# Attention of a decoder trunk: half of the last down group carried into the first attention steps, the first projection of a group issued after the last scores, and the end reordered

## The chip, the cores and the metric

The kernel runs on one core of a Trainium2 chip. The time is the device time of one execution in microseconds (us). Before the change the median of 3 runs is 2696.46 us (2696.24 to 2699.46). TensorE (PE) multiplies, VectorE (DVE) and ScalarE (ACT) do element work, GpSimd (POOL) helps them, and SyncE (SP) issues most transfers.

## The reference, cut to what matters

Two decoder layers over 1024 tokens of width 1024. The first mixes tokens by retention, the second by sliding-window attention; each is followed by a squared-ReLU MLP with 4096 hidden columns. The change lies in the seam between the MLP of layer 0 and the attention of layer 1, in the attention, and in the seam from it to the MLP of layer 1.

```
h = rmsnorm(x, norm_mix[1])
q, k, v = split(h @ w_in)                # 16 query heads in 4 groups, one key/value head per group, 64 wide
q = rope(rmsnorm(q, q_gain)); k = rope(rmsnorm(k, k_gain))
scores = q k^T * 64**-0.5, masked to the current and the previous block of 128 keys
probs = softmax([scores, sink])[..., :-1]
x = x + (probs @ v) @ w_out
h = rmsnorm(x, norm_mlp[1])
x = x + square(relu(h @ w_up)) @ w_down
```

## The kernel before, in words

Everything is float32. A product of two matrices is three matmuls (`product`, L475 to L483): each operand is split into a rounded part (hi, written by ACT) and a remainder (lo, written by DVE), and hi*hi, lo*hi and hi*lo are summed in PSUM. The residual stream xT lies transposed in SBUF: 8 pieces of 128 features by 1024 tokens, handled as 16 tiles of 128x512; tiles 0 to 7 are the first half of the tokens, tiles 8 to 15 the second.

The engines run their own instruction lists in the order written in the code, and wait for each other by counting semaphores. So the order of the work is written out by hand, and an instruction that waits holds up all behind it on its engine.

**Down groups.** An MLP's second matrix is applied in 16 groups of 256 hidden columns. A group is 16 tiles: `down` (L638) makes 6 matmuls of 512 columns on PE, `add` (L648) adds the result to xT on DVE. In the last group of layer 0 (`finish_dve`, L654) the next RMSNorm starts too: for each tile ACT writes hT_hi (L521) and a square (L516), DVE hT_lo (`norm_low`, L527), and POOL sums the squares (`norm_pool`, L535), 7 adds for each half. A few tiny matmuls sum over the partitions (`norm_stat_pe`, L544), and `norm_rstd` on DVE makes the reciprocal root in 10 small steps, each of which waits for the one before; other work is put between them.

**Attention.** `sw_steps` runs 4 groups of 8 blocks (128 queries each). The work on a block is cut into stages, and step s of a group runs the stages of several blocks:

- a (block s): 24 matmuls of 384 columns, the projection of q, k and v. ACT then squares and copies it (L1850, L1857, L1860), DVE takes the variance of each head and its root (L1964 to L1973, L463 to L473) and scales it (L1981, L1987), POOL rotates it (L2007 to L2017).
- b (block s-1): 4 transposes, after the rotation. ACT and DVE split the result (L1875, L1876, L1908, L1909).
- c (block s-1): 6 matmuls of 512 columns, the scores. DVE masks them and takes the row maximum (L1929, L1938, L1945 to L1949), ACT the exponentials (L1891, L1893), DVE the sum and a scaling (L1955, L1957, L2023), ACT the other half of the scaling (L1867).
- d, e (block s-2): 8 transposes and 12 matmuls of 256 columns, the weighted values (L1883, L1915, L1901, L2029).
- f (from s = 6 on, 2 tiles per step, also in the next group's first six steps): a down group with the output matrix, each tile followed by an `add`.

At a group's step 0, stages b to f still work for the blocks 6 and 7 of the group before; that is called a turn here. There are three. Projection weights of the next group are split at step 7 (L1758, L1763), the output matrix at steps 4 and 6, on DVE before the adds and before the end of the softmax.

**The end.** In the last group f makes 4 tiles per step from step 6 on. Its tiles 0 to 7 are finished by step 7; the last two steps (TT and TT+1, `drain_pe`, `drain_act`, `drain_dve`, `between_*`) finish the softmax of the last blocks, start the MLP of layer 1 (`p_pe`, `edge_act`, `edge_low`) and do tiles 8 to 15. Then `plain_act`, `plain_dve` and `up_pe` do the first eight results of the up product in the order `P_ORDER`; the norm's factor goes to memory and is read back broadcast (`rb_sp`), and the first ReLUs (`p_relu_dve`, L849) wait for it. The up product goes on (`u_pe`) once four ReLUs have freed a bank.

Of the kernel before, what the change touches and what calls it, by code (L numbers as in the profile page):

```python
# [85 lines left out]
P_ORDER = ((11, 0), (21, 0), (11, 1), (12, 0), (22, 0), (21, 1), (12, 1), (22, 1))  # L86
# [41 lines left out]
def trunk(nc, x_in, positions, norm_mix, norm_mlp, w_up, w_down, ret_in, ret_out, sw_in, q_gain,  # L128
          k_gain, sinks, sw_out, c_ident, c_causal, c_mask, c_head, c_freq, c_freq_row, out, y_dram, x_dram, a_dram, r_dram):
    ctx = ExitStack()  # L130
    with ctx:
# [365 lines left out]
        def sq_slot(n, i):  # L497
            return squares[:, i % 2, :] if n == 3 else xn[:, 0, (i % 2) * HALF:(i % 2 + 1) * HALF]
# [31 lines left out]
        def norm_pool(pool, n, half):  # L530
            for k in range(1, KT):
# [3 lines left out]
                pool.tensor_tensor(ss_of(half), ss_of(half), sq_slot(n, i), ALU.add).then_inc(n_ss, 1)  # L535

        def norm_stat_pe(pe, n, half):
# [3 lines left out]
            for part in ((0, 1) if n % 2 else (half,)):  # L541
                for j in range(4):
                    c = 4 * part + j
                    last = pe.matmul(ps[:, BSTAT, c:c + 1], ss_of(part)[:, j * P:(j + 1) * P], causal[:, P - 1:P],  # L544
                                     start=True, stop=True)
            last.then_inc(n_st, 1)

        def norm_rstd(dve, n, half, meanwhile=()):
# [5 lines left out]
            else:  # L554
                dve.wait_ge(n_st, RS_AT[n] - 2 + half + 1)
                total = ps[:, BSTAT, cols]
# [96 lines left out]

        def finish_dve(dve, g, between):  # L654
# [324 lines left out]
        def plain_dve(dve, layer, begin):  # L979
# [7 lines left out]
            for kk in range(4):  # L987
                t_dve(dve, layer, 6, kk)
            norm_rstd(dve, 2 * layer + 1, 0, [lambda kk=kk: b_lo_dve(dve, layer, 6, kk) for kk in range(4)] +
# [5 lines left out]
            p_lo_dve(dve, layer, 7)  # L995
# [17 lines left out]
        def plain_act(act, layer, begin, final):  # L1013
# [5 lines left out]
            for i in (5, 6):  # L1019
                for kk in range(4):  # L1020
                    b_hi_act(act, layer, i, kk, final)
            p_hi_act(act, layer, 7)
# [140 lines left out]
        def dn_pe(pe, layer, g, b, tile_done=None):  # L1163
            pe.wait_ge(w_lo, wc(PC_D[layer]) + 4 * g + 4)
            for m in range(TILES):
# [6 lines left out]
        def down_pe(pe, layer, tile_done):  # L1172
# [4 lines left out]
            dn_pe(pe, layer, D_LAST, 1, tile_done)  # L1177
# [590 lines left out]
        def a_pe(pe, g, t):  # L1768
            i = TT * g + t
            if t == 0:  # L1770
                pe.wait_ge(w_lo, WC_SW + SW_PIECES * g + 4)
                if isinstance(g, int) and g == 0:
                    pe.wait_ge(x_add, TILES * DG_SW - 3)
# [7 lines left out]
        def b_pe(pe, g, t):  # L1781
# [3 lines left out]
            if isinstance(g, int) and g == SW_KV - 1 and t >= TT - 2:  # L1785
                pe.wait_ge(x_add, TILES * (DG_SW + g) + 4 * (t - TT + 3))
            else:
                wait(pe, x_add, TILES * DG_SW + 2 * max(i - 5, 0) if isinstance(i, int) else TILES * DG_SW + 2 * (i - 5))
# [15 lines left out]
        def d_pe(pe, g, t):  # L1804
            i = TT * g + t
            pe.wait_ge(sw_prob, 2 * (i + 1))
            for s in range(2):
                wait(pe, sw_plo, 2 * (i - 1) + s + 1)
                for hh in range(4):
# [3 lines left out]
        def e_pe(pe, g, t):  # L1813
# [3 lines left out]
            if isinstance(g, int) and i == 0:  # L1817
                pe.wait_ge(n_var, 5)
# [9 lines left out]
        def f_pe(pe, g, q, c):  # L1828
            if c == 0:
                pe.wait_ge(sw_olo, TT * g + 4 * (q // 4) + 4)  # L1830
# [87 lines left out]
        def mask_half(dve, g, t, j):  # L1918
# [4 lines left out]
            if isinstance(g, int) and i == 0 and j == 0:  # L1923
                dve.wait_ge(sw_mask, 16)
                dve.wait_ge(n_ss, sums(2, 1, KT - 1))
# [108 lines left out]

        def drain_pe(pe, s):
# [12 lines left out]

        def drain_act(act, s):
            if s == TT - 1:  # L2050
                act.wait_ge(a_mm, TT * SW_KV)
                for m in range(4):
# [491 lines left out]
```

## Time and profile before

| | |
|---|---|
| median of 3 runs | 2696.46 us |
| the profiled execution's own time | 2694.79 us |
| its span, first to last instruction | 2693.1 us |
| mean granted TensorE clock | 0.982 of 2.4 GHz |
| PE busy | 2581.0 us (96%) |
| DVE busy | 1794.4 us (67%) |
| ACT busy | 931.8 us (35%) |
| POOL busy | 289.0 us (11%) |

The attention takes about 430 us of the span, from 1566 to 2008 us. The page is an average over stages with different limits; the change touches only the stretch from 1544 to 2062 us, so the stretches and single instructions there are what is to be read. Matmul rows overlap: a row's duration is longer than the distance to the next (0.39 against 0.227 us for 512 columns), so the starts are to be used.

### The profile page before, as it was taken

To read this page: it belongs to the slowest core of one execution; us is meant where nothing else is said; L and a number is where in the kernel's file an instruction comes from. 1 tells how busy PE (TensorE), PEld (TensorE's weight loads), DVE (VectorE), ACT (ScalarE), POOL (GpSimd) and SP (SyncE) were. 2 spreads that over 40 slices of the span, in tenths; PEclk is the share of its full clock that TensorE was granted. 3 is DMA by queue.
4 is the path that set the end of the run, shared out by engine and by line. 5 is a ranking of instruction groups with operands and counts; after the bars stand their busy time and mean duration, and the time that the engine had idled before them with its cause. 6 is when DMAs were issued, how large, how long until landed. Compare 5 with 4: busy or idle time off the path is not lost.

```text
span 2693.1 us, 36897 instructions
## 1 busy us (share of the span) xinstructions
PE 2581.0 (96%) x11929; PEld 2153.9 (80%) x11929; DVE 1794.4 (67%) x3397; ACT 931.8 (35%) x1732; POOL 289.0 (11%) x344
## 2 busy tenths in 40 slices
PE   8999999999999999999999988999888999999999
PEld 6878878878788888877888877888767888788887
DVE  7555454454667876666667788888867666576675
ACT  6232332322312544431112255555554444321111
POOL 2102011020000300000000043322320000000000
PEclk8999999999999999999999999999989999999999
DMA  6012120121333333343222201001113323522222
GB/s 206 28 48 67 52 68 16 48 71 47 134 101 97 116 123 117 119 150 121 95 100 93 87 21 40 17 24 40 35 52 118 125 90 112 195 94 99 96 93 86
DMA packets 161735, 231.77 MB, mean 86 GB/s; under 512 B 21681, under 2 KB 103889, under 8 KB 161618
## 3 DMA queue, kind: packets, MB, share of 16 engines
q1 hardware_dynamic: 159314, 226.10, 25.5%
q10 hardware_dynamic: 2304, 4.20, 0.4%
q8 instruction: 63, 1.03, 0.2%
q14 instruction: 54, 0.44, 0.0%
HBM read 171.53 MB, written 58.73 MB: 85 GB/s over the span
## 4 chain that ended last, share of the span: by engine, by line
PE 79%; DVE 11%; issue 5%; ACT 3%; DMA 1%; POOL 0%; DVEq 0%; ACTq 0%; SPq 0%
PE ps L480 25%; PE ps L482 25%; PE ps L481 25%; ACT xn L1891 1%; DVE xT L652 1%; DVE wqg_lo L449 1%; PE ps L1286 1%; PE ps L1287 1%; PE ps L1288 1%; DVE hT_lo L527 1%; DVE smax L1938 1%; DVE pT_lo L1915 1%; DVE hss L1971 1%; PE ps L1334 0%; DVE ws_lo L1763 0%
## 5 line engine op out<-in xcount | busy, mean ns | idle before, releaser
L652 DVE TENSOR_TENSOR xT<-ps,xT 128x512 f32<-128x512 f32 x704 | 482.1, 689 | 269.5 <-PE ps L482 269.2
L480 PE MATMUL ps<-aT_hi,wd_hi 128*128 128x512 f32 x1408 | 557.1, 396 | 21.9 <-DVE xT L652 19.3
L481 PE MATMUL ps<-aT_lo,wd_hi 128*128 128x512 f32 x1408 | 552.5, 392 | 0.0
L482 PE MATMUL ps<-aT_hi,wd_lo 128*128 128x512 f32 x1408 | 552.3, 392 | 0.0
L480 PE MATMUL ps<-bh,uw_hi 128*128 128x512 f32 x880 | 344.1, 391 | 10.3 <-DVE uw_lo L740 8.6
L482 PE MATMUL ps<-bh,uw_lo 128*128 128x512 f32 x880 | 343.4, 390 | 0.0
L481 PE MATMUL ps<-bl,uw_hi 128*128 128x512 f32 x880 | 343.3, 390 | 0.0
L480 PEld LDWEIGHTS ps<-aT_hi,wd_hi 128*128 128x128 f32 x1408 | 266.7, 189 | 79.9 <-issue 12.8
L482 PEld LDWEIGHTS ps<-aT_hi,wd_lo 128*128 128x128 f32 x1408 | 266.6, 189 | 56.1
L481 PEld LDWEIGHTS ps<-aT_lo,wd_hi 128*128 128x128 f32 x1408 | 266.8, 190 | 53.8
L442 ACT ACTIVATE aT_hi<-raw 128x1024 fp32r<-128x1024 f32 x80 | 80.8, 1052 | 604.8 <-PE ps L482 591.4
L480 PEld LDWEIGHTS ps<-bh,uw_hi 128*128 128x128 f32 x880 | 165.8, 188 | 45.9 <-DVE uw_lo L740 9.2
L481 PEld LDWEIGHTS ps<-bl,uw_hi 128*128 128x128 f32 x880 | 165.8, 188 | 34.1
L482 PEld LDWEIGHTS ps<-bh,uw_lo 128*128 128x128 f32 x880 | 165.6, 188 | 34.2
L1551 DVE BATCH_NORM_STATS2 bn<-ps 128x6 f32<-128x512 f32 x32 | 22.4, 699 | 157.0 <-PE ps L482 157.0
L1891 ACT ACTIVATE xn<-xn,nmax 128x256 f32<-128x256 f32 x128 | 63.6, 499 | 143.3 <-DVE sdif L1949 143.3
L758 DVE TENSOR_TENSOR uw_lo<-raw,uw_hi 128x512 fp32r<-128x512 f32 x112 | 77.0, 690 | 52.3 <-ACT uw_hi L753 51.5
L449 DVE TENSOR_TENSOR aT_lo<-raw,aT_hi 128x1024 fp32r<-128x1024 f32 x80 | 97.3, 1218 | 15.1 <-ACT aT_hi L442 15.1
L758 DVE TENSOR_TENSOR uw_lo<-us,uw_hi 128x512 fp32r<-128x512 f32 x84 | 58.0, 692 | 73.7 <-ACT uw_hi L753 73.7
L480 PE MATMUL ps<-wqg_hi,hT_hi 128*128 128x512 f32 x256 | 100.2, 391 | 4.9 <-DVE wqg_lo L449 4.9
L480 PE MATMUL ps<-wv_hi,hT_hi 128*128 128x512 f32 x256 | 102.2, 399 | 0.0
L480 PE MATMUL ps<-ws_hi,hT_hi 128*128 128x384 f32 x256 | 88.7, 347 | 11.7 <-DVE ws_lo L1763 6.7
(285 smaller groups left out, 4709.5 us busy)
## 6 DMA issues: line engine op xcount, KB each, us to landing
raw<-in_w_up SPq DMA_DIRECT2D x64, 512.0 KB, 6.0
raw<-in_w_down SPq DMA_DIRECT2D x64, 512.0 KB, 3.5
raw<-a_dram SPq DMA_DIRECT2D x64, 512.0 KB, 3.2
raw<-in_ret_w_in SPq DMA_DIRECT2D x48, 512.0 KB, 5.3
a_dram<-upost SPq DMA_DIRECT2D x64, 256.0 KB, 2.1
a_dram<-xn SPq DMA_DIRECT2D x64, 256.0 KB, 2.0
xT<-x_dram SPq DMA_DIRECT2D x24, 512.0 KB, 5.9
y_dram<-xn SPq DMA_DIRECT2D x32, 256.0 KB, 2.3
```

Source lines behind the costliest of these rows:

```text
L442: act.activation(dst, src, ACT.Copy).then_inc(w_hi, 1)
L449: dve.tensor_tensor(dst, src, hi.bitcast(F32), ALU.subtract).then_inc(w_lo, 1)
L480: pe.matmul(bank, ah, bh, start=(begin and i == 0), stop=False, skip_group_check=not begin)
L481: pe.matmul(bank, ah, bl, start=False, stop=False, skip_group_check=not begin)
L482: last = pe.matmul(bank, al, bh, start=False, stop=(i == len(pairs) - 1), skip_group_check=not begin)
L527: dve.scalar_tensor_tensor(hT_lo[:, k, cols], xT[:, k, cols], gain(2, k), hT_hi[:, k, cols].bitcast(F32), ALU.mult, ALU.subtract).then_inc ...
L652: dve.tensor_tensor(xT[:, k, cols], ps[:, banks[m % len(banks)], :], xT[:, k, cols], ALU.add).then_inc(x_add, 1)
L758: dve.tensor_tensor(uw(uw_lo, s % URING), weight(i, q), uw(uw_hi, s % URING).bitcast(F32), ALU.subtract).then_inc(u_lo, 1)
L1286: pe.matmul(bank, wh, hT_hi[:, k, cols], start=(k == 0), stop=False)
L1287: pe.matmul(bank, wh, hT_lo[:, k, cols], start=False, stop=False)
L1288: last = pe.matmul(bank, wl, hT_hi[:, k, cols], start=False, stop=(k == KT - 1))
L1891: act.activation(prob[:, hh, :, :], prob[:, hh, :, :], ACT.Exp, bias=nmax[:, hh:hh + 1], accum_out=ssum[:, hh:hh + 1]).then_inc(sw_exp, 1)
```

## The change

It has five parts.

1. **Start.** PE does only tiles 0 to 7 of the last down group of layer 0 before the attention. Tiles 8 to 15 use two PSUM banks of their own (`FILL`) and stand in the attention's steps 0 and 1 of group 0 (`first_steps_pe`): 8 to 10 ahead of the first projection, 11 behind it, 12 to 15 between the stages of step 1. Their norm work follows in steps 0 to 2, and the second half's statistics move from step 1 to step 3. The squares of this norm lie in unused halves of `raw`.
2. **Turn.** At step 0 of groups 1 to 3 the projection stands behind the scores of block 7 instead of first, with what follows from it on ACT and DVE; the two adds of f go between the steps of the root.
3. **Splits.** The two splits of the output matrix at steps 4 and 6 stand behind the end of the softmax on DVE.
4. **End.** f keeps 2 tiles per step through step 7. The end then has tiles 4 to 7 in step TT, and in step TT+1 pairs of the tiles 8 to 15 with halves of the up product between them. ACT squares tiles 0 to 7 along with tiles 8 to 15 and tiles 8 to 15 after them.
5. **Up.** `P_ORDER` swaps results 5 and 6 (both layers), and in layer 1 the last piece of plain weights (number 7) is split before the norm's root.

```diff
-P_ORDER = ((11, 0), (21, 0), (11, 1), (12, 0), (22, 0), (21, 1), (12, 1), (22, 1))
+P_ORDER = ((11, 0), (21, 0), (11, 1), (12, 0), (22, 0), (12, 1), (21, 1), (22, 1))
...
         def finish_dve(dve, g, between):
-            def one(m):
+            for m in range(KT):
                 add(dve, g, m)
-                if 4 <= m < 4 + KT:
-                    norm_low(dve, m - 4)
+                if m >= 2:
+                    norm_low(dve, m - 2)
                 between(m)
-            for m in range(13):
-                one(m)
-            norm_rstd(dve, 2, 0, [lambda m=m: one(m) for m in range(13, TILES)])
+            for m in (KT - 2, KT - 1):
+                norm_low(dve, m)
+            for m in range(KT, KT + 3):
+                add(dve, g, m, FILL)
+            norm_rstd(dve, 2, 0, [lambda m=m: norm_low(dve, m) for m in range(KT, KT + 3)])
...
+        def first_steps_pe(pe, s):
+            if s == 0:
+                for m in range(KT, KT + 3):
+                    fill_pe(pe, m)
+                norm_stat_pe(pe, 2, 0)
+                a_pe(pe, 0, 0)
+                fill_pe(pe, KT + 3)
+            if s == 1:
+                a_pe(pe, 0, 1)
+                fill_pe(pe, KT + 4)
+                b_pe(pe, 0, 0)
+                fill_pe(pe, KT + 5)
+                c_pe(pe, 0, 0)
+                fill_pe(pe, KT + 6)
+                fill_pe(pe, KT + 7)
...
         def drain_pe(pe, s):
             if s == TT:
-                pe.wait_ge(sw_vlo, TT * SW_KV)
-                p_pe(pe, 1, 0, (0,))
-                pe.wait_ge(sw_masked, 2 * TT * SW_KV - 1)
-                p_pe(pe, 1, 1, (0,))
-            if s == TT + 1:
+                b_pe(pe, LAST, TT - 1)
+                d_pe(pe, LAST, TT - 2)
+                c_pe(pe, LAST, TT - 1)
+                e_pe(pe, LAST, TT - 2)
+                for m in range(4, KT):
+                    drain_tile(pe, m)
+            else:
+                d_pe(pe, LAST, TT - 1)
+                pe.wait_ge(sw_vlo, TT * SW_KV)
+                for r in range(2):
+                    p_pe(pe, 1, r, (0,))
+                e_pe(pe, LAST, TT - 1)
+                p_pe(pe, 1, 2, (0,))
                 pe.wait_ge(sw_olo, TT * SW_KV)
-                p_pe(pe, 1, 2, (0,))
-                for m in range(KT, TILES):
-                    down(pe, DG_SW + SW_KV - 1, m, 1, BDS)
-                p_pe(pe, 1, 2, (1,))
+                for r in range(3):
+                    for m in (KT + 2 * r, KT + 2 * r + 1):
+                        drain_tile(pe, m)
+                    p_pe(pe, 1, r, (1,))
+                for m in (TILES - 2, TILES - 1):
+                    drain_tile(pe, m)
...
             def step(g, s, last_group):
                 begins = isinstance(g, int) and g == 0
+                turn = s == 0 and not begins
                 if which == "pe":
-                    run(a_pe, g, s, 0)
+                    if not turn:
+                        a_pe(eng, g, s)
...
                     run(lambda *a: f_pe(*a, 0), g, s, FLAG)
                     run(c_pe, g, s, 1)
+                    if turn:
+                        a_pe(eng, g, s)
                     run(lambda *a: f_pe(*a, 1), g, s, FLAG)
                     run(e_pe, g, s, 2)
```

The rows below are instructions in the order in which an engine has them; a name pair is result<-operands.

ACT at the turn into group 1, before: sq and copy are `scr` and `qk_raw`, `vp_hi` is the values' part, `xn,ssum` the exponentials.

```order
L1850 ACTIVATE scr<-ps,rstd 128x320
L1872 ISA
L125 ISA
L1875 ACTIVATE qT_hi<-ps 128x256
L1876 ACTIVATE kT_hi<-ps 128x2x128
L1857 ACTIVATE qk_raw<-ps,rstd 128x320
L125 REGISTER_ALU
L1860 ACTIVATE vp_hi<-ps,rstd 128x64
```

ACT at the same place in the changed kernel, from the two halves of pT_hi on:

```order
L1900 ACTIVATE pT_hi<-ps 128x512
L1905 REGISTER_ALU
L1908 ACTIVATE xn,ssum<-xn,nmax 128x256 x4
L1910 ACTIVATE esink<-sdif 128x4
L1860 ISA
L1867 ACTIVATE scr<-ps,rstd 128x320
L1874 ACTIVATE qk_raw<-ps,rstd 128x320
L125 REGISTER_ALU
L1877 ACTIVATE vp_hi<-ps,rstd 128x64
```

The three copies of the new projection have moved behind the five exponentials of the block before.

DVE at step 4 of group 0, before: `wd_lo` are the two splits of the output matrix, `xn<-xn,rden` is the scaling that ends the softmax.

```order
L1987 TENSOR_TENSOR scr<-scr,sins 128x320
L1763 TENSOR_TENSOR wd_lo<-raw,wd_hi 128x512 x2
L2029 TENSOR_TENSOR aT_lo<-ps,aT_hi 128x2x128
L1955 TENSOR_TENSOR den<-ssum,esink 128x4
L1957 RECIPROCAL rden<-den 128x4
L2023 TENSOR_TENSOR xn<-xn,rden 128x512
L1908 TENSOR_TENSOR qT_lo<-ps,qT_hi 128x256
```

DVE at the same place in the changed kernel:

```order
L2003 TENSOR_TENSOR scr<-scr,sins 128x320
L2045 TENSOR_TENSOR aT_lo<-ps,aT_hi 128x2x128
L1971 TENSOR_TENSOR den<-ssum,esink 128x4
L1973 RECIPROCAL rden<-den 128x4
L2039 TENSOR_TENSOR xn<-xn,rden 128x512
L1780 TENSOR_TENSOR wd_lo<-raw,wd_hi 128x512 x2
L1925 TENSOR_TENSOR qT_lo<-ps,qT_hi 128x256
```

The splits have moved behind the scaling, in front of the next block's qT_lo. The same holds at step 6 and in the later groups.

ACT at the end, before, from the last down tile's piece on (`squares` are squares of the norm, `h` and `bh<-ut` inputs of the up product made from all of xT):

```order
L919 ACTIVATE bh<-xT,gT 128x512
L516 ACTIVATE squares<-xT 128x512
L735 ACTIVATE uw_hi<-raw 128x512
L946 ACTIVATE h<-xT,gT 128x512 x4
L931 ACTIVATE bh<-ut 128x512 x8
L735 ACTIVATE uw_hi<-raw 128x512
```

ACT at the same place in the changed kernel:

```order
L929 ACTIVATE bh<-xT,gT 128x512
L520 ACTIVATE squares<-xT 128x512
L520 ACTIVATE xn<-xT 128x512
L520 ACTIVATE squares<-xT 128x512 x7
L745 ACTIVATE uw_hi<-raw 128x512
L956 ACTIVATE h<-xT,gT 128x512 x4
L941 ACTIVATE bh<-ut 128x512 x4
L745 ACTIVATE uw_hi<-raw 128x512
```

One square stood behind the last `bh`; now nine stand between it and `uw_hi`. The last `uw_hi` (plain weights 7) has moved between the two halves of `bh<-ut`.

## Rows read from the trace of the kernel before

**Rows 1.** Stretches: us, busy us of PE, PEld, DVE, ACT, POOL; granted clock, DMA, GB/s

```profile
1682.00:1716.10 34.10, 33.94 (x199) 30.36 (x197) 29.37 (x93) 17.59 (x58) 10.53 (x21) 1.00 0.00 1
1936.80:1988.00 51.20, 33.24 (x152) 27.75 (x152) 32.79 (x80) 22.86 (x59) 10.57 (x16) 0.79 0.18 62
```

**Rows 2.** Timeline, PE, group 1, f of three steps: start, us, engine, line, [idle before]

```profile
1705.00 0.48 PE L480 MATMUL ps<-aT_hi,wd_hi 128*128 128x512 f32 x1
...
1716.36 0.48 PE L480 MATMUL ps<-aT_hi,wd_hi 128*128 128x512 f32 x1
...
1729.33 0.48 PE L480 MATMUL ps<-aT_hi,wd_hi 128*128 128x512 f32 x1
```

**Rows 3.** Timeline, DVE, step 6 of group 0 and the block after

```profile
1649.80 1.96 DVE L1763 TENSOR_TENSOR wd_lo<-raw,wd_hi 128x512 fp32r<-128x512 f32 x2
...
1655.51 0.42 DVE L1908 TENSOR_TENSOR qT_lo<-ps,qT_hi 128x256 fp32r<-128x256 f32 x1 [1.21 <-ACT kT_hi L1876]
```

**Rows 4.** Timeline, PE, the turn into group 1

```profile
1660.91 0.28 PE L482 MATMUL ps<-pT_hi,vp_lo 128*128 128x256 f32 x1
1663.43 0.45 PE L480 MATMUL ps<-ws_hi,hT_hi 128*128 128x384 f32 x1 [2.24 <-DVE ws_lo L1763]
...
1669.12 0.43 PE L1791 MATMUL ps<-ident,scr 128*128 128x128 f32 x2 [1.25 <-POOL kr L2017]
...
1673.45 0.39 PE L480 MATMUL ps<-aT_hi,wd_hi 128*128 128x512 f32 x1
...
1680.77 0.43 PE L1791 MATMUL ps<-ident,scr 128*128 128x128 f32 x2 [0.19 <-issue]
```

**Rows 5.** Timeline, DVE, scaling of block 7 of group 0

```profile
1665.62 0.49 DVE L1981 TENSOR_TENSOR scr<-qk_raw,hrs 128x320 f32<-128x320 f32 x1
```

**Rows 6.** Timeline, DVE and ACT, a last mask and the last exponential behind it

```profile
1988.07 0.69 DVE L1929 SCALAR_TENSOR_TENSOR xn<-ps,swmask 128x512 f32<-128x512 f32 x1 [0.59 <-PE ps L482]
...
1992.44 0.19 ACT L1893 ACTIVATE esink<-sdif 128x4 f32<-128x4 f32 x1
```

**Rows 7.** Timeline, ACT, DVE and PE, block 0 of group 0

```profile
1573.95 0.53 ACT L1850 ACTIVATE scr<-ps,rstd 128x320 f32<-128x320 f32 x1 [2.48 <-DVE rstd L473]
...
1577.98 0.49 DVE L1981 TENSOR_TENSOR scr<-qk_raw,hrs 128x320 f32<-128x320 f32 x1
...
1583.42 0.44 PE L1791 MATMUL ps<-ident,scr 128*128 128x128 f32 x2
```

**Rows 8.** Timeline, PE, 12 matmuls after an idle time, and what follows them

```profile
1948.38 0.77 PE L480 MATMUL ps<-aT_hi,wd_hi 128*128 128x512 f32 x1 [5.66 <-DVE xT L652]
...
1953.37 0.28 PE L480 MATMUL ps<-pT_hi,vp_hi 128*128 128x256 f32 x1
```

**Rows 9.** Timeline, DVE, last down group of layer 0

```profile
1559.55 1.57 DVE L527 SCALAR_TENSOR_TENSOR hT_lo<-xT,gT,hT_hi 128x512 fp32r<-128x512 f32 x1
...
1561.64 0.74 DVE L527 SCALAR_TENSOR_TENSOR hT_lo<-xT,gT,hT_hi 128x512 fp32r<-128x512 f32 x1
...
1567.04 0.92 DVE L464 TENSOR_SCALAR rstd<-rstd 128x4 int32<-128x4 int32 x1
...
1573.67 0.16 DVE L473 SCALAR_TENSOR_TENSOR rstd<-rtmp,rstd 128x4 f32<-128x4 f32 x1
```

**Rows 10.** Timeline, POOL, one add of the same norm

```profile
1559.28 1.29 POOL L535 TENSOR_TENSOR xn<-xn 128x512 f32<-128x512 f32 x1 [0.80 <-ACT xn L516]
```

**Rows 11.** Timeline, the end: last add, last square, root, waiting matmul, fourth ReLU

```profile
2020.07 0.68 DVE L652 TENSOR_TENSOR xT<-ps,xT 128x512 f32<-128x512 f32 x1
...
2021.42 0.62 ACT L516 ACTIVATE squares<-xT 128x512 f32<-128x512 f32 x1
...
2034.38 0.17 DVE L557 TENSOR_SCALAR var<-ps 128x8 f32<-128x8 f32 x1 [1.39 <-PE ps L544]
...
2045.78 0.80 PE L480 MATMUL ps<-bh,uw_hi 128*128 128x512 f32 x1 [8.55 <-DVE uw_lo L740]
...
2059.29 0.68 DVE L849 SCALAR_TENSOR_TENSOR xn<-ps,scr 128x512 f32<-128x512 f32 x1
```

More of the change, by code:

```diff
@@ L535, in norm_pool, with stat_bank @@
                 pool.tensor_tensor(ss_of(half), ss_of(half), sq_slot(n, i), ALU.add).then_inc(n_ss, 1)
+        def stat_bank(n, half):
+            return 7 if n == 2 and half == 1 else BSTAT
         def norm_stat_pe(pe, n, half):
@@ L1161, in trunk, with dn_pe @@
         D_BUF = (2, 1)
-        def dn_pe(pe, layer, g, b, tile_done=None):
+        def dn_pe(pe, layer, g, b, tile_done=None, tiles=range(TILES)):
             pe.wait_ge(w_lo, wc(PC_D[layer]) + 4 * g + 4)
-            for m in range(TILES):
+            for m in tiles:
                 if isinstance(g, int) and g == 0 and m in (0, 2):
@@ L1176, in down_pe @@
                 dn_pe(pe, layer, 2 * gg + 2, 2)
-            dn_pe(pe, layer, D_LAST, 1, tile_done)
+            dn_pe(pe, layer, D_LAST, 1, tile_done, range(TILES if tile_done else KT))
         def down_act(act, layer, after):
@@ L1784, in b_pe @@
             wait(pe, sw_qlo, 2 * i)
[L1785 to L1788, printed above, removed]
+            if not isinstance(i, int) or i > 5:
+                pe.wait_ge(x_add, TILES * DG_SW + 2 * (i - 5))
             krf = kr[:, :, :].rearrange("p a d -> p (a d)")
@@ L2182, in step @@
-                    if s == TT - 1 and not last_group:
-                        splits = [lambda j=j: sw_split_lo(eng, g + 1, j) for j in range(4)]
-                        work = lows + splits[:2] + masks[:2] + splits[2:] + masks[2:]
-                    else:
-                        work = lows + masks
-                    if s < TT:
+                    if begins and s == 1:
+                        fill_dve(eng, KT + 5)
+                    masks = softmax(g, s)
+                    if turn:
+                        for w in lows(g, s) + masks:
+                            w()
+                        vlo_dve(eng, g, s)
+                        var_dve(eng, g, s)
+                        scale_dve(eng, g, s, out_adds(g, s))
+                    else:
+                        vlo_dve(eng, g, s)
+                        var_dve(eng, g, s)
+                        if s == TT - 1 and not last_group:
+                            splits = [lambda j=j: sw_split_lo(eng, g + 1, j) for j in range(4)]
+                            work = lows(g, s) + splits[:2] + masks[:2] + splits[2:] + masks[2:]
+                        else:
+                            work = lows(g, s) + masks
+                        if begins and s == 0:
+                            work = [lambda: fill_dve(eng, KT + 3)]
@@ L2188, in step @@
                         scale_dve(eng, g, s, work)
[L2189 to L2191 removed]
+                        for w in out_adds(g, s):
+                            w()
+                    if begins and s == 1:
+                        for m in (KT + 6, KT + 7):
+                            fill_dve(eng, m)
+                    run(oT_dve, g, s, 2)
+                    run(den_dve, g, s, 1)
+                    run(prob_dve, g, s, 1)
@@ L2222, in sw_steps @@
             group(SW_KV - 1, True)
-            for s in range(TT, TT + 2):
-                step(SW_KV - 1, s, True)
+            drain = {"pe": drain_pe, "act": drain_act, "dve": drain_dve}.get(which)
+            for s in (TT, TT + 1):
+                if drain:
+                    drain(eng, s)
         def table(dve, count, base, angle, turn, work, quarter):
```

241 lines of the change are left out of this document (135 added, 106 removed).

## The prediction

> **What bounds the kernel now.** Read the stretches first. In the steady attention PE is busy for 33.94 of 34.10 us at full clock, DVE for 29.37 [rows 1]: PE sets the pace there, and DVE has about 1.5 us free per step. In the stretch at the end of the attention PE is busy for 33.24 of 51.20 us at a clock of 0.79 [rows 1]: something else sets it. Then read the starts of PE's stages. A plain step takes 1716.36 - 1705.00 = 11.36 us, one with the splits of step 4 takes 1729.33 - 1716.36 = 12.97, that is 1.61 more [rows 2]. Last read the idle times: 2.24 us before the projection at a turn and 1.25 us before the transposes b behind it [rows 4], 8.55 us before the sixth result of the up product [rows 11]. Below, b7 are the transposes of a group's last block and b0 those of the next group's first.
>
> **Splits: 9.6 us gained.** They now stand behind the scaling that ends the softmax. DVE is idle there for 1.21 us until qT_lo [rows 3], because b and ACT come between. A pair of splits takes 1.96 us where POOL works beside it [rows 3]; behind the scaling POOL is through with its rotation, and two operations of about 0.6 us fill the idle time almost exactly. There are 8 places; the one at step 6 of group 3 is counted with the end. Five more lie in steps full of PE work (1.61 each), and two in group 0 where PE waits in any case, which I take at half: 5 x 1.61 + 2 x 0.8 = 9.65. Ends: 6 (the pairs overrun the idle time) and 11.3 (7 x 1.61).
>
> **Turns: 25.5 us lost.** The new place looks harmless to PE, which now waits 2.24 us for the new weights. But b7 waited for POOL's rotation of block 7, not for the projection: the projection ended some 1.3 us before [rows 4]. Nothing in the change makes that rotation earlier, as the splits of the new weights are still in step 7. So b7 keeps its time, the idle time before it grows from 1660.91 + 0.22 to 1669.12, 8.0 us, and the projection (24 matmuls, 4.2 us) leaves an idle time for a chain. From b7 to b0 it now reads:
> - b7 to the end of the scores: 1673.45 - 1669.12 = 4.3 us [rows 4];
> - 0.3 to the last mask, from it to the end of the last exponential 1992.44 + 0.1 - 1988.07 = 4.5 [rows 6], as ACT has the new projection's copies behind the exponentials; the projection itself ends earlier, at 8.5;
> - the copies, variance and root of block 0: 1577.98 - 1573.95 = 4.0 [rows 7], and two adds of 0.6 inside the root = 1.2;
> - scaling and rotation: 1669.12 - 1665.62 = 3.5 [rows 4, 5].
>
> Sum 17.8 us, where it was 1680.77 - 1669.12 = 11.65 [rows 4]: 6.2 us more. After it the steps are full again, so nothing is caught up. On top comes the clock. After 5.66 us of idle time 12 matmuls took 4.99 us instead of 12 x 0.227 = 2.72, their durations 0.63 to 0.80 instead of 0.39 [rows 8]: the granted clock was at the lower of its two levels, 1.2 GHz, and a restart cost 2.3 us. The 8.0 us are longer, and b7, f and the scores lie on the chain. One turn costs 8.5, three 25.5. Ends: 12 (no restart, and 4 us each, if part of the adds and copies overlap) and 32.
>
> The Trainium skill, page "TensorE: Matmul & The Clock Gate", section "Why this matters for your kernels", says to leave no idle gaps between bursts of matmuls because the array falls back to half its clock. The trace agrees at the 5.66 us gap. With it the turns come to 25.5, without it to 18.6.
>
> **Start: 0.** Before, DVE is the bound from the first add of the last group to the root at 1573.83 [rows 9]. The change takes 5 adds out from before the root (5 x 0.6) and puts 3 hT_lo in (3 x 0.66), and the root's small steps, of which several took 0.9 instead of 0.2 beside POOL [rows 9], are beside fewer POOL adds: by hand the root comes 3.6 us earlier. b of block 0, at 1583.42 before [rows 7], comes 4.7 earlier, as 5 hT_lo fewer stand beside the rotation. It is given back in step 1: ACT has two norm pairs (4 x 0.63) and a wait for a POOL add between the softmax and the next split, 2.7 us; POOL has four adds of 1.29 [rows 10] beside DVE's chain, and hT_lo took 1.57 beside such an add and 0.74 alone [rows 9], so 0.8 each in the worst case, of which one or two fall on the chain: 1.2; the second root moves to where DVE has less room than it needs, 0.7. 4.7 - 4.6 = 0.1, taken as 0. Ends: 4 gained, 5 lost. PE is half idle ahead of the first projection; a restart there is 2.3 of the 5.
>
> The Trainium skill, page "SBUF — State Buffer", section "SBUF: two separate sides", calls the port pair of VectorE and GpSimd an exclusive lock that the other waits out in full. By it all four POOL adds could cost 1.29 each, 5.2 us; the trace's 1.57 against 0.74 is less than that, and no add on PSUM data is stretched. The sum would be 4 us worse.
>
> **End: 9.0 us gained.** The old stretch holds 51.20 - 33.24 = 18 us of idle PE [rows 1], and three restarts of 2.3. Adds in fours, behind the masks on DVE, make the 5.66 us wait [rows 8]. The new order takes these away. Waits come back: before b7 there is no projection to fill PE, 3.3 us; before the last scores, 1.8; for the adds of tiles 4 and 5, 0.9; one restart, 2.3. So the last add (2020.07 before [rows 11]) comes 24.9 - 8.3 = 16.6, about 17 us earlier. But the end of the chain is not PE. Before, the last square began 1.35 us after the last add [rows 11]. Now ACT has nine squares behind the last add, of which seven are added up by POOL, 1.29 each and more beside DVE, with two buffers: ACT is free 10.3 us after the last add instead of 2.0, and the same chain of ACT and DVE work (h, ut, bh; 11 us) starts 8.3 us later relative to it. The split of plain weights 7 adds 0.6; 1.4 us of wait for the statistics [rows 11] drop out. Root: 17 - 7.6 = 9.4 us earlier. From the root to the end of the fourth ReLU it stays 2059.97 - 2034.38 = 25.6 us, most of it the factor's way through memory. PE had its eight results by 2061.9 (60 matmuls of 0.227 from 2045.78, and a restart of 2.3), 1.9 after that ReLU, and will now stand waiting for it, with a restart of 2.3: 9.4 + 1.9 - 2.3 = 9.0. The 8.55 us before the sixth result [rows 11] vanish for nothing, since they turn into this wait. Ends: 4 (POOL 1.7 per add beside DVE, two more restarts) and 17.
>
> **Up in layer 0: 0.** The swapped results' weights were ready; no idle time is there.
>
> **Sum.** -9.6 + 25.5 + 0 - 9.0 = +6.9 us on the profiled execution's 2694.79, so 2701.7. The median of the runs is 1.67 above that execution: 2703.4. Changes within 0.2%, 5.4 us, are about what a measurement of this kernel can't tell from none; my forecast lies just outside.
>
> **Rivals.**
> - *The end keeps what PE gains (not slower).* If the squares do not pile up on POOL, or the chain behind them has slack that I don't see, the end gives 17 instead of 9: 2695.4. For it: POOL is idle for most of this stretch. Against it: one POOL buffer pair and a fixed order on ACT. It decides from the point where ACT is free within 3 us of the last add.
> - *The turns pay no restart.* Then they cost 18.6 and the time is 2696.5. For it: at the turn into group 1 the 2.24 us gap left no trace. Against it: the 5.66 us gap did, and this one is 8.0 [rows 8].
> - *The turn does what it looks like.* If b7 were held by the projection's wait, it would come earlier and the turns cost nothing: 2677.9. Against it: POOL is named as the releaser of b7, 1.25 us after PE was free [rows 4].
> - *The start loses, and the half clock lasts longer (slower still).* The worst end of the start and 1 us more per turn: +8, 2711.
>
> **How the numbers follow.** Forecast 0.45 (own range 2698 to 2708), end keeps all 0.15, no restart 0.15, turn free 0.07, slower still 0.18. Slower by over 0.2% is above 2701.9: the last case and two thirds of the forecast, 0.48. Faster, below 2691.1: the free turn and the lower tails of the first two rivals, 0.16. Within: 0.36. The range 2688 to 2713 leaves out half of the free turn's case and the far tails.
>
> **What would show it.** In the changed profile: b7 comes some 16 us after b6, as before, with about 8 us of idle PE ahead of it, and slow matmuls after; b0 comes 17 to 20 us after b7. The steps with splits take 11.4 instead of 13.0. PE's waits near the end shrink to a few us each, and one of about 14 us stands ahead of the up product's second round, released by a ReLU. ACT's squares are spaced by POOL's adds. Steps of group 0 from the third on start at about the same time as before. I am wrong if b7 moves by more than its splits' 1.6 us, if the turn's chain is under 14 us, or if the root at the end comes over 13 us earlier relative to the start of step 6.

## The result, and the profile after

The changed kernel takes 2704.89 us (median of 8 runs, 2702.72 to 2706.03), the kernel before 2696.35 us beside it (8 runs, 2693.47 to 2700.83). The ratio is 1.0029 (95% interval 1.0018 to 1.0039): 8.5 us slower. The prediction was 2703.4. The profiled execution took 2702.72 us, its span is 2701.1 us.

The stretches of [rows 1] after the change (us, busy us of PE, PEld, DVE, ACT, POOL; granted clock, DMA, GB/s), and one behind the first wait of a turn:

```profile
1682.00:1716.10 34.10, 31.70 (x178) 28.65 (x177) 26.61 (x86) 15.53 (x47) 10.96 (x21) 0.95 0.00 1
1936.80:1988.00 51.20, 45.64 (x246) 39.68 (x245) 46.36 (x134) 30.26 (x93) 13.13 (x27) 0.93 0.21 71
...
1668.50:1674.10 5.60, 5.60 (x25) 5.08 (x26) 2.92 (x6) 2.34 (x6) 0.00 (x0) 0.73 0.00 0
```

The second stretch has filled up: 45.64 busy us where there were 33.24. Part of that is another piece of the work, as the group comes later now; from b of block 5 to the last add it is 2018.74 - 1952.04 = 66.7 us after the change and was 2020.07 - 1936.79 = 83.3. The first stretch, full before, now holds a wait, and behind the wait of a turn the granted clock is 0.73, between its two levels of 1.2 and 2.4 GHz. PE's timeline at the first turn, which answers to [rows 4]:

```profile
1660.29 0.28 PE L482 MATMUL ps<-pT_hi,vp_lo 128*128 128x256 f32 x1
1668.50 0.69 PE L1804 MATMUL ps<-ident,scr 128*128 128x128 f32 x2 [7.93 <-POOL kr L2033]
...
1669.40 1.91 PE L1825 MATMUL ps<-ident,xn 128*128 128x128 f32 x8
1670.97 0.72 PE L480 MATMUL ps<-aT_hi,wd_hi 128*128 128x512 f32 x1
...
1672.67 0.39 PE L480 MATMUL ps<-kT_hi,qT_hi 128*128 128x512 f32 x1
...
1674.04 0.33 PE L480 MATMUL ps<-ws_hi,hT_hi 128*128 128x384 f32 x1
...
1687.72 0.44 PE L1804 MATMUL ps<-ident,scr 128*128 128x128 f32 x2 [2.36 <-POOL kr L2033]
```

The last exponential of block 7 on ACT and the scaling of block 0 on DVE, between the scores and b0:

```profile
1678.71 0.19 ACT L1910 ACTIVATE esink<-sdif 128x4 f32<-128x4 f32 x1
...
1683.75 0.49 DVE L1997 TENSOR_TENSOR scr<-qk_raw,hrs 128x320 f32<-128x320 f32 x1
```

The transposes of block 7 (b7) start at 1668.50, 0.6 us from their time before, with 7.93 us of idle PE ahead. From them to the next group's first (b0) it is 1687.72 - 1668.50 = 19.2 us instead of 11.65. The other two turns have 20.2 and 19.7.

The steps with splits: b of blocks 5 and 6 of group 1 were 12.14 us apart, since the 1.61 of [rows 2] spread over two steps, and are now 1756.95 - 1745.57 = 11.38 apart:

```profile
1745.57 0.33 PE L1804 MATMUL ps<-ident,scr 128*128 128x128 f32 x1
...
1756.95 0.32 PE L1804 MATMUL ps<-ident,scr 128*128 128x128 f32 x1
```

The start. DVE's first split of the new weights, ahead of all that is changed but the order of the up product in layer 0, stands at 1544.69 in the profiled execution before and at 1543.11 after:

```profile
1544.69 1.22 DVE L1763 TENSOR_TENSOR ws_lo<-raw,ws_hi 128x1024 fp32r<-128x1024 f32 x1
```

```profile
1543.11 1.22 DVE L1780 TENSOR_TENSOR ws_lo<-raw,ws_hi 128x1024 fp32r<-128x1024 f32 x1
...
1578.67 0.44 PE L1804 MATMUL ps<-ident,scr 128*128 128x128 f32 x2 [0.79 <-POOL kr L2033]
...
1591.93 0.63 ACT L520 ACTIVATE raw<-xT 128x512 f32<-128x512 f32 x1 [1.66 <-POOL xn L539]
...
1595.77 0.50 PE L480 MATMUL ps<-kT_hi,qT_hi 128*128 128x512 f32 x1 [3.97 <-DVE kT_lo L1926]
...
1621.05 0.79 PE L480 MATMUL ps<-kT_hi,qT_hi 128*128 128x512 f32 x1 [2.60 <-DVE kT_lo L1926]
1621.64 0.63 PE L481 MATMUL ps<-kT_lo,qT_hi 128*128 128x512 f32 x1
```

So 1.58 us are due to what came before, and must be taken off (this is called a run's offset below): b of block 0 is 4.75 - 1.58 = 3.2 us earlier than in [rows 7], not 4.7. Then two waits ahead of the scores of blocks 1 and 3 take it back. Without such a hold the wait ahead of the scores is 0.67 us (e7 below). The second is followed by matmuls of 0.63 us.

The end, beside [rows 11]: last add, two of the squares behind it, root, fourth ReLU, and the matmul that waits for it (the first of the up product's second round).

```profile
2018.74 0.69 DVE L659 TENSOR_TENSOR xT<-ps,xT 128x512 f32<-128x512 f32 x1
...
2022.97 0.64 ACT L520 ACTIVATE squares<-xT 128x512 f32<-128x512 f32 x1 [1.06 <-POOL xn L539]
...
2030.15 0.63 ACT L520 ACTIVATE squares<-xT 128x512 f32<-128x512 f32 x1 [0.80 <-POOL xn L539]
...
2041.32 0.15 DVE L564 TENSOR_SCALAR var<-ps 128x8 f32<-128x8 f32 x1
...
2064.31 0.68 DVE L859 SCALAR_TENSOR_TENSOR xn<-ps,scr 128x512 f32<-128x512 f32 x1
...
2065.14 0.76 PE L480 MATMUL ps<-bh,uw_hi 128*128 128x512 f32 x1 [10.28 <-DVE xn L859]
2065.70 0.63 PE L481 MATMUL ps<-bl,uw_hi 128*128 128x512 f32 x1
```

From the last add to the root it was 14.3 us and is 22.6. Squares come 1.43 us apart, each released by POOL. After 10.28 us of waiting, PE starts at 0.63 us per matmul instead of 0.39.

Added up between the two profiled executions: b0 of groups 1, 2, 3 comes 6.95, 12.14, 17.10 us later than before, the last block 5 (behind one more pair of splits) 15.25 later, the last add 1.33 earlier, the root 6.94 later, the fourth ReLU 5.02 later, DVE's work in the up product behind the restart 7.13 later, the end 8.0 later.

### The profile page after: what moved, and what is told of

Its sections match the earlier page's. It is cut to its first block, busy times and chain, and to the rows that moved or that the text cites. A ratio compares the mean times of both kernels' runs of the same rounds, so it can differ in the third digit from the quotient of the medians.

```text
span 2701.1 us, 36897 instructions
## 1 busy us (share of the span) xinstructions
PE 2583.7 (96%) x11929; PEld 2157.6 (80%) x11929; DVE 1787.0 (66%) x3397; ACT 933.6 (35%) x1732; POOL 282.1 (10%) x344
## 4 chain that ended last, share of the span: by engine, by line
PE 80%; DVE 9%; issue 5%; ACT 3%; POOL 1%; DMA 0%; DVEq 0%; POOLq 0%; ACTq 0%; SPq 0%
PE ps L480 25%; PE ps L482 25%; PE ps L481 25%; ACT xn L1908 2%; DVE wqg_lo L449 1%; DVE smax L1954 1%; PE ps L1303 1%; PE ps L1305 1%; PE ps L1304 1%; POOL xn L539 1%; DVE hss L1987 0%; DVE pT_lo L1932 0%; PE ps L1351 0%; PE ps L1335 0%; DVE ws_lo L1780 0%
## 5 line engine op out<-in xcount | busy, mean ns | idle before, releaser
L482 PE MATMUL ps<-wv_hi,hT_lo 128*128 128x512 f32 x256 | 99.8, 390 | 0.0
```

Source lines behind the costliest of these rows:

```text
L482: last = pe.matmul(bank, al, bh, start=False, stop=(i == len(pairs) - 1), skip_group_check=not begin)
```

## Experiments

All times are medians beside runs of the kernel before. Two kernels whose medians are under some 2 us apart are not told apart by that alone.

**e1: the turns as before.**

```diff
-                turn = s == 0 and not begins
+                turn = False
```

> The changed kernel with the turns as before (projection of the next group first in step 0). My theory: the turns cost 25.5 us by the prediction's sum; the trace of the changed kernel has the first transposes of the groups 1, 2 and 3 6.8, 5.2 and 5.0 us later against the kernel before, and 3.2 us of gained splits per group hidden in the last two, so about 8.3 each. So 2704.9 - 25 = 2680, between 2677 and 2684. Rival 1, the turns pay no restart: 18.6, so 2686. Rival 2, the turn is harmless and the loss is elsewhere: 2705.

Measured: 2680.66 us (2677.27 to 2681.95), ratio to before 0.9945 (0.9932 to 0.9958). The turns cost 24.2 us; without them the change is a gain. In the two traces, from b6 of one group to b1 of the next, they cost 9.0, 7.5 and 8.0.

**e3: the kernel before, with only the turns changed** (projection behind the scores, its work on ACT and DVE behind the exponentials and masks).

```diff
-                    run(a_pe, g, s, 0)
+                    if not turn:
+                        run(a_pe, g, s, 0)
...
                         run(c_pe, g, s, 1)
+                        if turn:
+                            a_pe(eng, g, s)
```

> The kernel before with only the turns changed. My theory: 3 by 8.5 = 25.5 us lost, 2696.4 + 25.5 = 2722 (2718 to 2725). Rival 1, the matmuls behind the idle time at half clock do not lie on the chain: 18.6, so 2715. Rival 2, the turn costs only together with the other parts of the change: under 2706.

Measured: 2721.56 us (2717.67 to 2722.07), ratio 1.009 (1.0077 to 1.0103): 25.4 us. The turn costs the same alone as with the rest, so no other part causes or softens it as far as these medians tell.

**e2: the kernel before, with only the splits moved.**

```diff
-                    if s in (4, 6):
-                        for j in range(s, s + 2):
-                            sw_split_lo(eng, g, j)
...
                     run(prob_dve, g, s, 1)
+                    if s in (4, 6):
+                        for j in range(s, s + 2):
+                            sw_split_lo(eng, g, j)
```

> The kernel before with only the splits of steps 4 and 6 moved behind the end of the softmax. My theory: 5 steps by 1.61 and 2 by 0.8, and the one at step 6 of group 3: 9.6 us gained, 2696.4 - 9.6 = 2686.8 (2685 to 2690). Rival, a pair of splits only changes its place on a DVE that is the bound there: same time, 2696.4 within 1.5.

Measured: 2684.06 us (2682.75 to 2685.11), ratio 0.9957 (0.9945 to 0.997): 12.1 us gained, just outside the range expected. The 9.6 of the expectation is without the pair at step 6 of group 3, which the prediction counts with the end; with its 1.61 the sum is 11.3.

**e8: changed turns, with the splits of the new projection weights behind them.** They stood on DVE ahead of the scaling of block 7.

```diff
                     if turn:
+                        for j in range(4):
+                            sw_split_lo(eng, g, j)
...
-                        if s == TT - 1 and not last_group:
-                            splits = [lambda j=j: sw_split_lo(eng, g + 1, j) for j in range(4)]
-                            work = lows(g, s) + splits[:2] + masks[:2] + splits[2:] + masks[2:]
-                        else:
-                            work = lows(g, s) + masks
+                        work = lows(g, s) + masks
```

> The changed kernel (turns as changed) with the four splits ws_lo of the new projection weights moved on DVE from step 7, between the masks and the root of block 7, to the turn, behind kT_lo of block 7. Tests the step of the prediction that the transposes of block 7 are held by POOL's rotation and this by the splits ahead of the scaling. My theory: they come 3.6 us earlier in each turn, PE's idle time falls from 7.9 to 4.3, and the chain behind them grows by about 1 as the masks wait for the splits: 2704.9 - 3 x 2.6 = 2697 (2694 to 2700). Rival, the transposes are held by something else or the chain grows by all of it: 2704.9 within 2.

Measured: 2700.11 us (2697.05 to 2703.17), 4.8 less than the changed kernel, where 7.8 were expected. PE at the first turn:

```profile
1655.36 0.39 PE L1804 MATMUL ps<-ident,scr 128*128 128x128 f32 x2
...
1666.82 0.68 PE L1804 MATMUL ps<-ident,scr 128*128 128x128 f32 x2 [4.11 <-POOL kr L2033]
...
1688.12 0.44 PE L1804 MATMUL ps<-ident,scr 128*128 128x128 f32 x2 [2.88 <-POOL kr L2033]
```

b7 comes 11.46 us after b6 instead of 15.26, and the wait falls from 7.93 to 4.11: the splits did hold it, by way of POOL's rotation. The chain behind it grows from 19.2 to 21.3, twice what was expected, since the splits now delay block 7's masks: the first comes 7.3 us after b7 (DVE's timeline, 1674.08) instead of 5.1 (1673.56 in the changed kernel).

**e4: PE kept busy in the wait.** 38 matmuls whose result is not used stand ahead of b7.

```diff
+        def warm(g, n=38):
+            nc_pe = warm_eng[0]
+            wait(nc_pe, sw_vlo, TT * g)
+            for _ in range(n):
+                nc_pe.matmul(ps[:, SA, 0:SW_COLS], hT_hi[:, 0, 0:P], hT_hi[:, 0, 0:SW_COLS], start=True, stop=True)
...
+                    if turn:
+                        warm(g)
                     run(b_pe, g, s, 1)
```

> The changed kernel with 38 extra matmuls of 384 columns per turn in PE's idle time ahead of the transposes of block 7, into the bank that the next projection overwrites; their result is not used. They take about 38 x 0.177 = 6.7 of the 7.9 us. My theory: the clock stays at 2.4 GHz, so the restart of 2.3 us in each turn goes, and the chain of 17.8 stays: 2704.9 - 7 = 2698 (2696 to 2701). Rival 1, the slow matmuls run beside the chain of DVE, ACT and POOL: 2705 within 1.5. Rival 2, the extra matmuls themselves delay the transposes of block 7: slower than 2705.

Measured: 2702.76 us (2697.62 to 2705.82), 2.1 less than the changed kernel, where 7 were expected. It lies between the theory's range and that of the first rival; the ranges of the two kernels overlap, and the traces say more.

```profile
1670.26 0.43 PE L1805 MATMUL ps<-ident,scr 128*128 128x128 f32 x2 [1.31 <-POOL kr L2034]
...
1688.26 0.43 PE L1805 MATMUL ps<-ident,scr 128*128 128x128 f32 x2 [2.36 <-POOL kr L2034]
...
1690.85 0.63 PE L481 MATMUL ps<-aT_lo,wd_hi 128*128 128x512 f32 x1
```

b7 is fast (0.43 where it was 0.69) and comes 15.24 us after b6, so the extra matmuls do not delay it. The chain to b0 is 18.0, 19.0 and 18.0 us instead of 19.2, 20.2 and 19.7. So a restart is worth 1.2 to 1.7 us on that chain, 4.1 in all three, not 2.3 each. At the third turn a stretch of slow matmuls comes back behind b0: b0 to b1 takes 12.7 us instead of 11.1. At the first turn such matmuls stand behind b0, after 2.36 us of idle time, in both kernels.

**e6: turns and start as before**; what is left is splits, end and up. The diff of the start in the other direction, from e1:

```diff
-                    if begins and s < 2:
-                        first_steps_pe(eng, s)
-                        return
...
-                    if begins and s == 3:
+                    if begins and s == 1:
                         norm_rstd(eng, 2, 1)
```

> e1 with the start as before as well: what is left of the change is splits, end and up. It closes the sum: its difference from e2 (splits alone, 2684.1) is the end, its difference from e1 (2680.7) the start. My theory: the start is worth 0, so 2680.7 within 2, and the end 9 less the place of the splits at step 6, so 2684.1 - 7 = 2677 within 3. The two don't agree by 3; the trace of e1 has the transposes of block 7 in group 0 1.2 us later than e2 has, which speaks for 2678 to 2679. Rival, the start gains the 4 us by which its first block comes earlier: 2684 or more.

Measured: 2678.01 us (2676.67 to 2678.76), ratio 0.9927 (0.9914 to 0.9941). The start costs 2680.66 - 2678.01 = 2.7 us; the ranges overlap, but the traces agree: with each run's own offset (as above) taken off, b7 of group 0 is 1.95 us earlier than before in e6 and 0.2 later in e1. The end with the order of up gains 2684.06 - 2678.01 = 6.1 beyond the splits.

**e5: e1 with the squares earlier.**

```diff
                 prob_act(act, LAST, TT - 1)
+                for m in range(3):
+                    norm_square(act, 3, m)
...
                 for m in range(KT, TILES):
                     b_hi_act(act, 1, FROM_X[m // 4], m % 4, SW_FINAL)
-                    norm_square(act, 3, m - KT)
-                for m in range(KT, TILES):
                     norm_square(act, 3, m)
```

> e1 (the changed kernel with the turns as before) and the squares of the last norm as early as the tiles allow: 8 of them before the adds of tiles 8 to 15, then one per tile, so that one square and one POOL add stand behind the last add instead of nine and ten. My theory: in the changed kernel the root comes 22.6 us after the last add, against 14.3 before, because POOL's ten adds of 1.43 us hold ACT; so the root comes 8.3 us earlier, the 10.4 us wait ahead of the up product's second round shrinks to 2, and the time is 2680.7 - 8.3 = 2672.4 (2670 to 2675). Rival 1, something else ends last there (the matmuls that wait for bl, or the memory way of the factor): gain under 3, 2678 or more. Rival 2, squares among the matmuls' feeds delay the up product's inputs on ACT and move the last add: 2676 to 2680.

Measured: 2672.89 us (2670.2 to 2673.87), ratio 0.9908 (0.9893 to 0.9923): 7.8 us less than e1.

```profile
1999.75 0.69 DVE L659 TENSOR_TENSOR xT<-ps,xT 128x512 f32<-128x512 f32 x1
...
2013.10 0.17 DVE L564 TENSOR_SCALAR var<-ps 128x8 f32<-128x8 f32 x1 [0.29 <-PE ps L551]
...
2036.89 0.77 PE L480 MATMUL ps<-bh,uw_hi 128*128 128x512 f32 x1 [7.35 <-DVE xn L859]
```

The root comes 13.4 us after the last add instead of 22.6. It was 2018.04 - 1995.43 = 22.6 in e1 too. The time is as expected, but the wait is not: 7.35 us are left where 2 were expected, since PE's first round, no longer held for the statistics, is through earlier too.

**e7: e5 with the start mended.**

```diff
                     run(pT_act, g, s, 2)
+                    if begins and s == 2:
+                        for m in (KT + 6, KT + 7):
+                            last_norm_act(eng, m)
...
-                    if begins and s == 1:
-                        for m in (KT + 6, KT + 7):
-                            last_norm_act(eng, m)
...
+                    if begins and s == 3:
+                        norm_rstd(eng, 2, 1)
                     run(oT_dve, g, s, 2)
...
-                    if begins and s == 3:
-                        norm_rstd(eng, 2, 1)
```

> e5 with two things in the start moved: ACT's last two norm pairs stand behind the two halves of pT_hi in step 2 instead of at the end of step 1, where they wait 1.7 us for a POOL add behind the rotation and hold the split of block 1 back by 3.4; and the second root stands ahead of aT_lo in step 3, in DVE's 1.4 us of idle time, instead of behind the softmax, where it costs 2.0 and starts a stretch of half clock on PE. My theory: the waits of 3.97 and 2.60 us before the scores of blocks 1 and 3 shrink to about 0.7 each, 5 us gained against e5: 2667.5 if e5 is 2672.4. Rival, PE is full again after step 4 only because DVE paces group 0, and the waits come back in a later step: gain under 1.5 against e5.

Measured: 2670.32 us (2666.55 to 2670.61), 2.6 less than e5; the ranges touch.

```profile
1595.91 0.50 PE L480 MATMUL ps<-kT_hi,qT_hi 128*128 128x512 f32 x1 [0.67 <-DVE kT_lo L1926]
...
1621.82 0.50 PE L480 MATMUL ps<-kT_hi,qT_hi 128*128 128x512 f32 x1 [0.66 <-DVE kT_lo L1926]
```

Both waits shrank as expected, but 1.6 us appear ahead of b of block 2 and 1.4 ahead of the d of step 3: half of the 5 us stays. The median lies between the theory's 2667.9 and the rival's bound.

**e9 and e10: the last root earlier**, on e7 and on e6 with e5's squares.

```diff
-STAT_AT = (3, 5)
+STAT_AT = (3, 4)
...
+                norm_rstd(dve, 2 * layer + 1, 0, [lambda kk=kk: t_dve(dve, layer, 6, kk) for kk in range(4)] +
+                          [lambda: p_lo_dve(dve, layer, 7)] +
+                          [lambda kk=kk: b_lo_dve(dve, layer, 6, kk) for kk in range(4)])
```

> e7 with the last norm's root earlier: its statistics stand one result earlier on PE, and on DVE the root begins ahead of the four ut of the third combination, which go between its steps. In e5 the root came 13.4 us after the last add, though POOL had its sum 3.5 us after it. My theory: 7.4 us of PE's wait ahead of the up product's second round hang on the root; it comes 4 us earlier, and so do the fourth ReLU and that wait's end: 2670.3 - 4 = 2666 (2664 to 2668). Rival, the inputs made between the root's steps come later and PE loses it again in the first round: 2669 to 2672.

> e6 (start and turns as before) with the squares of e5 and the root of e9. My theory: the mended start of e7 and the start of before are worth the same, since e6 - 7.8 - 4 is 2666, as for e9. Rival, the start of before is still the better one by 2 us or more (e1 against e6 has 2.7): 2664 or less, or the mended one is: 2668 or more.

Measured: e9 2668.58 us (2666.77 to 2671.78), e10 2667.93 us (2665.43 to 2671.25). The ratios are 0.9896 (0.988 to 0.9913) and 0.9894 (0.9877 to 0.991): mended start and old start are worth the same within what medians of four runs tell. Against e7 the gain is 1.7 us, not 4, which the medians alone don't tell from none. In the traces the root begins 9.75 us after the last add (13.34 in e7) but ends only 1.3 us earlier, 17.9 against 19.2 after it. The expectation of e11 has 4.4 and 2.1 for this, without the offset. DVE in e9:

```profile
2004.28 0.15 DVE L564 TENSOR_SCALAR var<-ps 128x8 f32<-128x8 f32 x1
...
2008.70 0.69 DVE L750 TENSOR_TENSOR uw_lo<-raw,uw_hi 128x512 fp32r<-128x512 f32 x1 [1.27 <-ACT uw_hi L745]
...
2012.47 0.17 DVE L473 SCALAR_TENSOR_TENSOR rstd<-rtmp,rstd 128x8 f32<-128x8 f32 x1
```

A split that waits for ACT sits between its steps; the root takes 8.4 us.

**e11: e10 with only the four `ut` between the steps.**

```diff
-                          [lambda: p_lo_dve(dve, layer, 7)] +
-                          [lambda kk=kk: b_lo_dve(dve, layer, 6, kk) for kk in range(4)])
+                p_lo_dve(dve, layer, 7)
+                for kk in range(4):
+                    b_lo_dve(dve, layer, 6, kk)
```

> e10 with only the four ut between the root's steps; the split of plain weights and the four bl, which wait for ACT there, stand behind the root. In e9 the root began 4.4 us earlier than in e7 but ended only 2.1 earlier, since its steps stood behind such waits. My theory: it ends 3.5 to 4 us earlier than in e10 (2011.3 in its trace), and the wait ahead of the up product's second round shrinks from 6.4 to under 3: 2667.9 - 3.7 = 2664 (2662 to 2666). Rival, the splits and bl that come later feed the first round, and PE waits there: 2667 to 2670.

Measured: 2663.49 us (2662.52 to 2664.8), ratio 0.9881 (0.9864 to 0.9899): 32.8 us below the kernel before, the fastest version.

```profile
2005.29 0.15 DVE L562 TENSOR_SCALAR var<-ps 128x8 f32<-128x8 f32 x1
...
2009.24 0.17 DVE L473 SCALAR_TENSOR_TENSOR rstd<-rtmp,rstd 128x8 f32<-128x8 f32 x1
...
2027.63 0.47 PE L480 MATMUL ps<-bh,uw_hi 128*128 128x512 f32 x1 [2.29 <-DVE xn L855]
2027.94 0.40 PE L481 MATMUL ps<-bl,uw_hi 128*128 128x512 f32 x1
...
2029.13 0.63 PE L480 MATMUL ps<-bh,uw_hi 128*128 128x512 f32 x1
```

The root takes 4.1 us, and the wait ahead of the second round is 2.29 where it was 6.38 in e10. PE starts behind it at 0.47 and 0.40, but the restart is not gone: 1.5 us later come eight matmuls at 0.63. The first 20 matmuls behind the wait take 6.26 us, where 20 x 0.227 would be 4.54, so slow matmuls still cost 1.7 us. The gain is the earlier end of the wait.

## Why the prediction was right

| term | predicted | measured |
|---|---|---|
| splits | -9.6 | -12.1 (e2), of which 1.6 belong to the end's term: -10.5 |
| turns | +25.5 | +24.2 (e1), +25.4 (e3) |
| start | 0 | +2.7 (e1 against e6) |
| end and up | -9.0 | -6.1 (e6 against e2) and the 1.6: -7.7 |
| sum | +6.9 | +8.7 |

The measured column is made of steps from one kernel to the next (before, e2, e6, e1, changed), so its sum closes by construction; only e3 measures a term a second time.

The total is right because its two large terms are, the turns above all. That it is within 2 us is in part luck: splits and turns came out 0.9 and 1.3 us better than forecast, start and end 2.7 and 1.3 worse.

- **Turns.** Its core held: b7 hangs on the rotation behind DVE's splits, not on the projection. b7 kept its time at the first turn (0.6 us earlier in the profile, 1.0 later with the offset taken off), and e8, which moves the splits, brought it 3.8 us closer to b6. The prediction read this from the first turn alone. At the other two in the kernel before, the new projection itself ran slow and no wait stands ahead of b7; it came 16.2 and 16.1 us after b6 there, against 16.0 at the first, so this held it by 0.2 at most. The chain without restart is 18.0, 19.0 and 18.0 us (e4) against 17.8, and its parts fit too: at the first turn, with restart, 5.5 us to the end of the scores (4.3 predicted without it), 4.8 to the last exponential (4.8), 4.9 to the scaling (5.2), 4.0 to b0 (3.5). The restart was over-priced: 2.3 on the chain against 1.2 to 1.7. The trace of the kernel before could have told: behind the wait of 8.55 us [rows 11], seven matmuls took 2048.80 - 2045.78 = 3.0 us instead of 1.6, a restart of 1.4 where the row it went by has 2.3:

```profile
2048.07 0.63 PE L482 MATMUL ps<-bh,uw_lo 128*128 128x512 f32 x1
2048.50 0.46 PE L480 MATMUL ps<-bh,uw_hi 128*128 128x512 f32 x1
2048.80 0.40 PE L481 MATMUL ps<-bl,uw_hi 128*128 128x512 f32 x1
```

What made up for it is the chain without restart, 1.6 us longer over the three turns than forecast, and a second loss behind b0, which the prediction did not have: 1.4 us at the first turn (b0 is 6.95 later, b1 8.33). That they are about as large as the mistake is luck.
- **Splits.** As worked out. In e2, with the offset off, b7 of group 0 is 1.96 us earlier (1.6 predicted), and b5 of group 3 another 8.4 (five full steps, 8.05 predicted).
- **Start.** This step failed. The gain at b of block 0 was 3.2, not 4.7. Two prices were too low: ACT's norm pairs and their wait for a POOL add hold the next block's scores back by 3.97 - 0.67 = 3.3 us, as rotation and adds stand in line on POOL, against the 2.7 predicted; and the second root, which stands alone behind the softmax with nothing between its steps, takes 2.0 us and brings slow matmuls, against 0.7. e7, which moves just these two, takes the loss back. It lies within the ends given (5 lost). One reading of rows was wrong though it changed little: 1.57 against 0.74 us is no sign against the lock that the prediction quotes. POOL's add ends at 1559.28 + 1.29 = 1560.57 [rows 10], and hT_lo, begun at 1559.55 [rows 9], ends 0.55 after it, so it was stretched by what was left of the add.
- **End.** Last add 16.6 us earlier than block 5 would have it (15.25 + 1.33), predicted 16.6; from it to the root 8.3 us more, predicted 17 - 9.4 = 7.6, for the reason given: POOL's adds pace ACT's squares, and e5 takes 7.8 back. The term as a whole, 9.0 against 7.7, is off by less than these runs resolve; in the two traces the work behind the second round comes 15.25 - 7.13 = 8.1 us earlier than block 5 would have it. Two slips in its sum are small: 8.3 + 0.6 - 1.4 is 7.5 and not 7.6, and PE had its eight results by 2061.0, not 2061.9, again because the restart was over-priced. One row that it rests on was unlucky: the factor took 10.7 us to memory in the profiled execution before, 9.4 in the one after, and from root to fourth ReLU it was 24.9 there and 23.0 to 23.3 in the changed kernel and in e1 to e8. A wait of 14 us was forecast ahead of the up product's second round, it was 10.28 and 2.90 ahead of the statistics.
- **Up in layer 0.** No effect to be seen: the first split behind it stands at 1544.69, 1545.67 and 1546.32 in the three traces with the old order, and between 1543.11 and 1547.57 in the ten with the new one.

Of the rivals, "the turns pay no restart" was nearer to the truth in its mechanism than the chance of 0.15 says: in e4 the restarts are worth 4.1 us on the three chains and some 2 in the time, not 7. Its time was wrong since other losses fill the place. What the prediction had for it, that the gap of 2.24 us left no trace, holds for one turn of three; behind the gap of 2.23 us at the next one, eleven matmuls of 384 columns ran at 0.42 to 0.53 us instead of 0.34:

```profile
1761.68 0.50 PE L480 MATMUL ps<-ws_hi,hT_hi 128*128 128x384 f32 x1 [2.23 <-DVE ws_lo L1763]
1761.97 0.53 PE L481 MATMUL ps<-ws_lo,hT_hi 128*128 128x384 f32 x1
```

## What to carry to other kernels

When an engine waits twice in a row, ask what each wait's releaser hangs on before moving the work between them: here it only covered a wait that had another cause, and moving it made the wait 7.9 us and put 6 us of chain behind it. Work that fills the steps of a serial chain must be ready itself; an operation that waits for another engine makes the chain twice as long (8.4 us against 4.1). And a gain of several us is best kept out of one sum with a loss: the two parts that lost (turns, squares behind the last add) hid a gain of 23 us, which e5 has with the rest of the change as it is.

## What the runs showed of the hardware that was not expected

A wait of PE does not always cost a restart. At the first turn of the changed kernel matmuls took 0.63 us behind a wait of 2.36 us, and the granted clock of that stretch is 0.72. At the second turn the same stages follow a wait of 2.34 us at full speed, and in e11 (above) the slow matmuls come only 1.5 us after a wait of 2.29 us. The stretch, and PE at the two turns:

```profile
1688.00:1694.00 6.00, 6.00 (x27) 5.13 (x26) 4.08 (x13) 2.25 (x6) 0.87 (x1) 0.72 0.00 0
```

```profile
1690.01 0.63 PE L481 MATMUL ps<-aT_lo,wd_hi 128*128 128x512 f32 x1
...
1792.39 0.44 PE L1804 MATMUL ps<-ident,scr 128*128 128x128 f32 x2 [2.34 <-POOL kr L2033]
...
1793.98 0.39 PE L481 MATMUL ps<-aT_lo,wd_hi 128*128 128x512 f32 x1
```

Behind every wait of 3.9 us or more named here slow matmuls followed, at once or shortly after: b of the last block, after 3.9 us, took 0.69 in e6, and in e1 0.44, with slow matmuls from 0.8 us on. So the first matmul behind a wait does not tell whether a restart is paid; the rows that follow have to be read too. What decides at the waits between 2.2 and 2.9 us stays open. And executions of kernels that are the same up to the changed stretch, but for the order in layer 0, reach it up to 4.5 us apart (-1.58 in the changed kernel, +2.88 in e6, against the one before), so an edit's effect is read from times with this offset taken off.
